# Block 0's down projection by seven products, and its weight sums formed in DRAM

## The reference

```python
    h = h + jnp.concatenate([y_lru, y_pool], axis=-1) @ w_out[i]
    v = rms_norm(h, g_ffn[i])
    up = causal_dwconv(v @ w_up[i], w_conv_ffn[i], b_conv_ffn[i])
    gate = up[..., :D_FF]
    val = up[..., D_FF:]
    h = h + (jax.nn.gelu(gate) * val) @ w_down[i]
    q = rms_norm(h, g_ple[i])
```

## Time and profile before

| | before |
|---|---|
| device time, median of 3 runs | 2148.7 us (2148.31 to 2149.93) |
| span of the profiled execution | 2147.1 us |
| matmuls | 9296 |
| busy: PE, PEld, DVE, ACT, POOL | 2116.0, 1746.0, 1466.8, 867.6, 365.7 us |
| moved by DMA | 419.08 MB, 195 GB/s over the span |
| chain that ended last | PE 97%, DVE 1%, DMA 1% |

### The profile page before, as it was taken

The page is one execution under the profiler, slowest core; times in us unless marked ns, Lnnn a source line. Parts: engine busy times, 40 slices in busy tenths (PEclk is TensorE's granted clock), DMA queues, the critical chain, the costliest instruction groups (busy, mean ns, idle before and its releaser), DMA issues.

```text
span 2147.1 us, 24298 instructions
## 1 busy us (share of the span) xinstructions
PE 2116.0 (99%) x9296; PEld 1746.0 (81%) x9296; DVE 1466.8 (68%) x1679; ACT 867.6 (40%) x1128; POOL 365.7 (17%) x684
## 2 busy tenths in 40 slices
PE   8999999999999999999999999999999999999996
PEld 6888888888888888888888888888888888888884
DVE  7885497685858677688786743874655656574866
ACT  5764364352525344355445622522313131323342
POOL 0101002111112211221100111122222222222210
PEclk9999999999999999999999999999999999999998
DMA  5436546566657556576533364466666666666643
GB/s 223 162 142 261 179 167 242 203 250 218 243 193 268 220 212 235 218 288 245 191 124 135 98 215 131 145 191 193 194 194 192 194 195 195 190 194 196 211 152 108
DMA packets 134994, 419.08 MB, mean 195 GB/s; under 512 B 15456, under 2 KB 15584, under 8 KB 134880
## 3 DMA queue, kind: packets, MB, share of 16 engines
q0 software_dynamic: 91776, 318.81, 42.8%
q1 hardware_dynamic: 40800, 90.33, 12.8%
q10 hardware_dynamic: 2304, 8.39, 1.0%
HBM read 244.46 MB, written 173.02 MB: 194 GB/s over the span
## 4 chain that ended last, share of the span: by engine, by line
PE 97%; DVE 1%; DMA 1%; ACT 0%; SPq 0%; issue 0%; DVEq 0%; ACTq 0%
PE slot L660 47%; PE slot L807 38%; PE slot L887 11%; DMA XN<-xT 1%; PE slot L725 1%; DVE H L2159 0%; PE slot L738 0%; PE slot L749 0%; DVE wpair L1499 0%; DMA split_panels<-wpair 0%; DVE wsum L1493 0%; SPq L558 0%; DVE WV L2150 0%; DVE XQ L2154 0%; DVE WV L2152 0%
## 5 line engine op out<-in xcount | busy, mean ns | idle before, releaser
L807 PE MATMUL slot<-ops,wpair 128*128 128x512 f32 x3696 | 841.9, 390 | 0.7 <-ACT WG L1225 0.4
L807 PEld LDWEIGHTS slot<-ops,wpair 128*128 128x128 f32 x3696 | 693.6, 188 | 147.0 <-ACT WG L1225 3.0
L660 PE MATMUL slot<-Uhi,wpair 128*128 128x512 f32 x1248 | 339.7, 391 | 10.5 <-DVE wpair L1499 8.6
L620 POOL DMA_DIRECT2D split_panels<-wpair x274 | 146.1, 534 | 840.0 <-DVE wpair L1499 815.4
L660 PEld LDWEIGHTS slot<-Uhi,wpair 128*128 128x128 f32 x1248 | 234.7, 188 | 60.9 <-issue 9.5
L645 POOL DMA_DIRECT2D wpair<-split_panels x262 | 141.2, 539 | 753.0 <-PE slot L660 346.6
L660 PE MATMUL slot<-f_split,wpair 128*128 128x512 f32 x1152 | 262.1, 389 | 0.0
L660 PEld LDWEIGHTS slot<-f_split,wpair 128*128 128x128 f32 x1152 | 216.4, 188 | 44.7
L887 PE MATMUL slot<-f_quarter,wpair 128*128 128x512 f32 x1008 | 229.5, 389 | 0.0
L887 PEld LDWEIGHTS slot<-f_quarter,wpair 128*128 128x128 f32 x1008 | 189.3, 188 | 39.2
L965 ACT ACTIVATE wpair<-raw 128x512 fp32r<-128x512 f32 x186 | 113.4, 624 | 253.4 <-PE slot L660 168.2
(11 more groups left out here) (197 smaller groups left out, 2298.4 us busy)
## 6 DMA issues: line engine op xcount, KB each, us to landing
split_panels<-wpair POOLq DMA_DIRECT2D x274, 512.0 KB, 4.6
wpair<-split_panels POOLq DMA_DIRECT2D x262, 512.0 KB, 3.6
raw<-panels SPq DMA_DIRECT2D x208, 256.0 KB, 4.2
wpair<-down_sums POOLq DMA_DIRECT2D x48, 256.0 KB, 2.9
wlo_sum<-down_sums POOLq DMA_DIRECT2D x48, 256.0 KB, 3.0
down_sums<-raw POOLq DMA_DIRECT2D x36, 256.0 KB, 3.2
H<-xT SPq DMA_DIRECT2D x8, 1024.0 KB, 10.4
pp_kept<-XQ ACTq DMA_DIRECT2D x16, 512.0 KB, 3.7
```

The costliest lines, as they stand in the source:

```text
L620: pool.dma_start(split_d[n], wpair[n % RING][:].bitcast(F32)).then_inc(split_kept[n % RING], 16)
L660: mm = pe.matmul(ps[:, h * BANK:(h + 1) * BANK], stat_[:, w], mov(part, h), start=first and i == 0, stop=last and i == 2)
L807: mm = pe.matmul(ps, stat_[:, w], (lo if part else hi)[:, k, :], start=first and k == 0 and i == 0, stop=k == KP - 1 and i == 2, skip_grou ...
```

## The change

Block 0's down projection is done by the seven products too, from a different layout of f: block 0 has no room for the unsplit f tiles (their place is that of the raw buffers), so T2, T3 and T4 are formed by DVE from the split parts in WG, WV and AG, in seven instructions of 128 x 1024, and T1 piecewise in AV while the pairs run. The down projection of block 0 now takes 14 panels a chunk instead of eight, eight of them being sums. These sums are formed in DRAM by POOL's transfers: four copies and four accumulating transfers of 256 KB for each of 12 items, in 15 stages, one every four panels from panel 8 on, each waiting for the stage ahead. They are then loaded and split like any panel, and block 1 loads them split. The order of the products changes (P2 ahead of P6), T signs are turned (products are subtracted from H where they were added), and the statistics step `stat(b, 2)` moves behind the second gate tile in block 0. SP loads block 1's x in four parts between panels.

```diff
-DOWN_ORDER = (("P1", 0), ("P5", 0), ("P1", 1), ("P5", 1), ("P3", 0), ("P3", 1), ("P6", 0), ("P6", 1),
-              ("P2", 0), ("P2", 1), ("P7", 0), ("P7", 1), ("P4", 0), ("P4", 1))
+DOWN_ORDER = (("P1", 0), ("P5", 0), ("P1", 1), ("P5", 1), ("P3", 0), ("P3", 1), ("P2", 0), ("P2", 1),
+              ("P6", 0), ("P6", 1), ("P7", 0), ("P7", 1), ("P4", 0), ("P4", 1))
...
+                panel(key, raw(("sum", c, i, DOWN_SUMS[name]) if name in DOWN_SUMS else
+                               ("down", c, i, DOWN_PLAIN[name])))
...
-            if m == (1 if b else 0):
+            if m == 1:
                 stat(b, 2)
...
+            def sums_stage(at):
+
+                pool.wait_ge(sum_terms, 16 * 4 * min(at, len(SUM_ITEMS)))
+                if at >= 1:
+                    pool.wait_ge(sum_s1_s3, 16 * 2 * min(at - 1, len(SUM_ITEMS)))
+                if at >= 2:
+                    pool.wait_ge(sum_s2, 16 * min(at - 2, len(SUM_ITEMS)))
+                if 0 <= at - 3 < len(SUM_ITEMS):
+                    c, i = SUM_ITEMS[at - 3]
+                    pool.dma_start(sums_d[c, i, 3], sums_d[c, i, 1], accum_op=ALU.add, max_dma_last_dim=ADDED_ROW).then_inc(sum_s4, 16)
...
+                if at < len(SUM_ITEMS):
+                    c, i = SUM_ITEMS[at]
+                    for k, kind in enumerate(("21", "11", "11", "12")):
+                        pool.dma_start(sums_d[c, i, k], from_panel(c, i, kind)).then_inc(sum_terms, 16)
...
             for n in range(SPLIT):
                 pool.wait_ge(panel_lo, n + 1)
                 pool.dma_start(split_d[n], wpair[n % RING][:].bitcast(F32)).then_inc(split_kept[n % RING], 16)
...
+                at, rest = divmod(n - SUM_FIRST, SUM_EVERY)
+                if rest == 0 and 0 <= at < len(SUM_ITEMS) + SUM_STAGES - 1:
+                    sums_stage(at)
...
+            def t2_terms(b, c):
+
+                dve.wait_ge(d_ready, d_count(b, c, "T1"))
+                dve.wait_ge(f_ready, b * FT + c * CHUNK + CHUNK)
+                b22, t1 = ([f32(f_quarter[:, k, part, :, :]) for part in range(2)] for k in (3, 1))
+                chain.mark(v.tensor_tensor(d_whole("T2"), b22[0], t1[0], ALU.add))
+                return chain.mark(v.tensor_tensor(d_whole("T4"), b22[1], t1[1], ALU.add))
...
             def down_by_seven(b, c, q):
...
                 gate_conv(b, q)
+                refill(b, q, "P4")
                 val_conv(b, q)
                 f_tile(b, q)
-                sum_lo_part(b, c, "P5", 1)
+                weights(("P1", 0),)
+                down_added(b, c, "P5", 0, 1)
                 f_lo_tile(b, q)
...
+                weights(("P5", 0),)
+                if b == 0:
+                    terms = t2_terms(b, c)
+                    down_added(b, c, "P5", 2, 3)
+                    t2_whole(terms)
+                    down_added(b, c, "P1", 0, 1)
+                    weights(("P1", 1),)
+                    down_added(b, c, "P3", 0, 1)
+                    weights(("P5", 1),)
+                    formed = less_hi(b, c, "T3")
+                    down_added(b, c, "P3", 2, 3)
+                    less_lo(b, c, "T3", formed)
+                    down_added(b, c, "P1", 2, 3)
+                    weights(("P3", 0),)
+                    d_lo_half(b, c, "T2")
...
+                    formed = less_hi(b, c, "T4")
+                    if ends:
+                        down_added(b, c, "P2", 0, 1, 2, 3)
+                    down_added(b, c, "P6", 0, 1)
...
+                if not ends:
+                    down_added(b, c, "P7", 0, 1, 2, 3)
+                    if b == 0:
+                        down_added(b, c, "P2", 0, 1, 2, 3)
+                    weights(("P7", 0),)
+                    down_added(b, c, "P4", 0, 1)
+                    weights(("P7", 1),)
+                    down_added(b, c, "P4", 2, 3)
+                    weights(("P4", 0),)
                     return
```

More of the change, by code:

```diff
@@ L252 @@
 SPLIT = PANEL[1, "L", 0, 0]
-KEPT_AT, IN_COUNT, SUM_TURN = {}, {}, {}
+KEPT_AT, IN_COUNT = {}, {}
 def kept_panels():
@@ L1389, in ffn @@
[L1389 to L1401 removed]
+                    down_his(b, c)
@@ L1485, in wsummed @@
                         dve.wait_ge(*landed(r))
-                if n > PANEL[0, "down", 0, 0, "11"]:
-                    dve.wait_ge(first_sum_kept, 16 * 2 * sum(PANEL[0, "down", c, 0, "11"] < n for c in range(BY_SEVEN)))
                 if SUMS[n] > 1:
```

469 lines of the change are left out of this document (211 added, 258 removed).

## The result

The changed kernel takes 2190.55 us (median of 4 runs, 2188.81 to 2192.39) against 2149.07 for the kernel before (4 runs, 2148.31 to 2149.93): a ratio of 1.0192, 95% interval 1.0178 to 1.0207. It is slower, as forecast, but by 41.5 us where I said 20, and above the range's upper end of 2182. The profiled execution, the slowest of the four, spans 2190.5 us, 43.4 more than before.

A forecast was written before the change was run, and what follows sets the result against it. The prediction took the number of TensorE matmuls as the bound. Removing 144 (-32.6 us), waits in chunks 0 to 4 (+42.5) and chunk 5 with the gate (+10.4) gave +20.3: span 2167.4, forecast 2169 us, range 2130 to 2182.

The forecast's parts named there:

- The matmuls removed (-32.6): Block 0's down projection: 144 fewer matmuls at 0.2267 us each, 24 in each of 6 chunks, save 32.6 us.
- DVE in block 0 (6.5 + 2.0 a chunk): Chunks 0 to 4: TensorE loses 6.5 us waiting in the products and 2.0 at the handover, 42.5 in all.
- The walk: Instruction-by-instruction timing of a block 0 chunk's products from TensorE's first matmul: they end at 44.6 us instead of 38.1.
- Rival A: In block 0 DVE keeps up and TensorE never waits: 2116 us; chance 0.11.
- B: DVE's two 1.8 us idle spots in block 0's products are absent because ACT is ahead: 2148 us; chance 0.14.
- The spacing of 0.69 us for each 512-wide instruction: DVE instructions start 0.69 us apart, not 0.60: 1.7 us more a chunk, sum +30; this alone chance 0.03.
- Four panels pass between 60.57 and 81.83 ... I take nothing: Accumulating transfers on POOL: eight per stage against 21 us between stages; bounds nothing to 36 us, nothing taken.
- waits before 350 us: Sign against the forecast: TensorE's block 0 waits fall this early, then POOL or the transfers are responsible.
- rival D: Slower still, 2179 to 2205 us: POOL held by slow accumulates, late panel writes, or wider DVE instruction spacing; chance 0.15.
- The kept writes' 0.3 us of cover: Block 0: panel writes land 0.3 us ahead of T3's sum; landings 2 us later cost up to 12 us.
- Chunk 5 and the gate (+10.4, so +5.0 net): Block 0's end: four P2 adds ahead of P6's, and gate low halves sharing DVE with panel halves, cost 10.4 us.
- Block 1 at nothing: Block 1: 48 fewer low halves on DVE, changed order, larger loads; no new TensorE wait, no time change.

The follow-up runs named there:

- order edits: Against the changed kernel: two panels' low halves moved behind the f tiles on DVE, 2168.7 us; separately, P1's snapshot ahead of a panel's high half on ACT, 2184.25 us.
- half the transfers: The changed kernel without the 48 accumulating transfers and the waits for them, the 48 copies kept: 2178.9 us, ratio 1.0141.
- 2153.4 us kernel: The changed kernel with both DVE and ACT orders mended, eight sum stages in the first 26 panels and 39 transfers in stages behind panels 38 to 62: ratio 1.0018.
- T2's low half first: Against the 2153.4 us kernel: T3 formed right behind T2, P1's additions after T2's low half on DVE, T2's high half one panel earlier on ACT: 2153.0 us.

## Why the prediction was right in its mechanism and wrong in its size

**The matmuls removed (-32.6):** 144 fewer, as said.

**DVE in block 0 (6.5 + 2.0 a chunk): right.** The products of chunks 2 to 4 last 44.8 us for 44.6, the waits for f's and T2's low halves and the snapshot measured 2.08, 1.62 and 1.80 for 2.1, 2.0 and 2.0, and the period grew by 2.7 to 3.0 us for 3.06. The order edits then took away 21.9 and 6.3 us. The walk had no clock in it, and it mostly didn't matter: in chunk 2, 24 matmuls took 1.4 us longer behind the first wait, and the waits for additions shrank from chunk 1's 0.51 and 1.12 to 0.31, since DVE paced both. In chunk 1 the clock fell behind the handover instead, where nothing absorbs it: 312 matmuls in 72.65 us for 71.04, which is the 1.6 us by which its period (4.7) exceeds the forecast. Rival A fell (TensorE waits in every chunk), and so did B (both idle spots are there). The spacing of 0.69 us for each 512-wide instruction, which would have made the sum +30 and which the prediction set out by the Trainium skill, "VectorE: DVE Perf Modes", section on the TRN2 errata, is not borne out either, as the earlier trace rows had it: in chunk 2 the instruction behind the low half of 623.68 starts at 624.29, 0.61 us later.

**"Four panels pass between 60.57 and 81.83 ... I take nothing": this is the step that failed.** It cost 15.9 us before the first down projection, where the bounds were 0 and 36. I asked whether eight transfers fit between two stages, so whether POOL would be held up. They do fit: eight take 12.8 to 18.1 us from the first issue to the last landing, and the stages follow one another at the panels' pace (55.1, 76.6, 92.6, 118.0 us). The 21 us was read wrongly all the same, since 60.57 and 81.83 are the first and the fourth of four panels, and the 0.8 us at the low end of the bound has no row behind it. What I did not ask is who else uses the DMA engines then: the reload of x and p from 177 us on, behind which a panel took 18.2 us already before, and which a stage beside it made 25.0. The 36 us end was worked out and said to stay in the range, and then the range ended at 2182; the sentence that named waits before 350 us as what would prove me wrong named the place. The run that moved only the places shows that the places cost 11 to 12 us; with the order mended it is 6.8, and as the front alone varies by 4 us between executions, 7 to 12 us is what the runs carry. The adding has a share too, which overlaps with it: with plain copies at the change's places the first down projection is 8.7 us late (363.51), with half the transfers 3.2 (358.01). The time lies in rival D's range (2179 to 2205, 0.15), but not by its causes in the main: POOL was not held, and TensorE's two largest losses ahead of the first down projection came from a late load of a panel and a late write of `pp_kept`; late panel writes, which D names, show in chunk 0.

**The kept writes' 0.3 us of cover: gone in chunk 0 only.** There ACT waited 3.21 and 2.58 us for two writes (until 366.62 and 369.83 us), right behind the last stages, and TensorE's first wait in the products is 3.45 us instead of 2.08: the 1.4 us of its period (4.4) over the forecast.

**Chunk 5 and the gate (+10.4, so +5.0 net): undersized.** It is 6.5 + 2.4 net. The four P2 additions ahead of P6's were to show 1.7 us at P7 and measured 3.45 (at 1026.38), with the clock at 0.92 from 996 to 1040 us; 1.68 us stand at a gate panel's late low half.

**Block 1 at nothing: right in its products.** They still run at 0.2267 us a matmul, and no wait stands in them. Behind the last ones TensorE waits 0.43 us for a panel's load (at 2082.71), and the end is 0.7 us longer.

The terms: front 15.9 for 0, chunks 17.9 for 15.3, chunk 5 and the gate 8.9 for 5.0, end of block 1 0.7 for 0; together the 23.1 us of 43.4 - 20.3.

No version here beats the kernel before. The best three come to within 0.18 to 0.22% of it, slower by intervals that exclude zero. In their profiles a period from one down projection to the next is 118.3 to 119.0 us in the mean where eight products took 120.1, so 24 matmuls a chunk (5.4 us) buy 1.1 to 1.8. In the 2153.4 us kernel's profile the five periods win 5.4 us together; chunk 5 and the gate, where DVE has P2's additions and the gate's low halves as well, lose 5.2 of it, and the front 2.5. No run tried eight products in chunk 5 alone, and the rest of the front's loss was not taken apart.

## What to carry to other kernels

Traffic that fits by its mean share is not free: list what is loaded with little lead (here a reload of 4 MB with panels queued behind it, and panels in a ring of four), read the share of the DMA engines over just the time such a load is in flight (1.02 against 0.85 here, where 40 us gave 0.90 and 0.89), and keep extra transfers off those stretches, since the same 96 transfers cost 38 us more in one set of places than in another (2215.7 against 2178.1). When a matmul is traded for vector work, add up the vector engine's time within the stretch that uses its results; once it was full there, in the run with T2's low half first, a new order moved the wait and won nothing. Bounds that were worked out belong in the range unless a row excludes them.
